# Gate and up products of three feed-forward blocks: one product of 512 columns for the upper weights, parts added outside PSUM

## The chip, the cores and the metric

One Trainium2 chip, one of its cores. The metric is the device time of one execution in microseconds, as the median of several executions. The whole program is one launch; all engines work on one example of 256 tokens.

## The reference, cut to what matters

Two blocks of two layers each run one after the other on `x` (256 tokens of width 1024). Three of the feed-forward parts in it are plain gated blocks, and these are the ones touched:

```python
def swiglu(xn, w_gu, w_down):                      # first block, layer 0
    g, u = jnp.split(xn @ w_gu, 2, axis=-1)        # hidden width 2816
    return (jax.nn.silu(g) * u) @ w_down

# second block, both layers, hidden width 2816
xn = _rms_norm(x, ffn_norm[l])
gate = _causal_dwconv(xn @ ffn_w_gate[l], ffn_conv_w[l], ffn_conv_b[l])
x = x + (jax.nn.silu(gate) * (xn @ ffn_w_up[l])) @ ffn_w_down[l]
```

The rest (mixers, attention, a mixture of eight experts) is not touched.

## The kernel before, in words

All data is float32. To use the fast reduced type of TensorE (float32r) without its loss of precision, each operand is split into an upper half (the value rounded to float32r) and a lower half (the rest), and a product is the sum of three: upper weights with upper input, upper weights with lower input, lower weights with upper input (`passes`). A weight block of 128x2048 arrives by DMA in one of four `raw` buffers; ScalarE copies it to its upper half `wH` (`act_blocks`, the copy is L229), then VectorE subtracts to get the lower half `wL` (`dve_blocks`, L200). There are three buffers of halves, so a block's halves can only be written when TensorE has finished the block three places back. Both functions work three blocks ahead of the tag they are called with.

A gated block is `pe_glu` on TensorE, `act_glu` on ScalarE and `dve_glu` on VectorE. It goes over the hidden width in 11 rounds of 256 channels. Round r on TensorE is: gate product (`pe_two`, L796), up product (`pe_two`), then the down product of round r-1 (L780; the last one is `pe_down_last`, L806). Weight blocks come in the same order: gate r, up r, down r-1. In `pe_two` the weights are stationary (128x128) and the input is moving (256 tokens): for each of 2 column halves j and 8 chunks c of the width there are three products of 256 columns, 48 in all. Gate or up of a round fill one PSUM bank of 512 columns, half j at columns 256j. The banks of these products are taken in turn from the four of the span (4, 8); banks 0 to 3 hold the sum of the down products. `bank` makes TensorE wait for the instruction that freed the bank last time: `dve_two`, which reads the bank, multiplies by the token scale `inv` and writes to SBUF.

VectorE's order in a round (`dve_glu`): weight halves that are due, gate scale (and in the second block three convolution taps, `dve_conv_gate`), up scale, product with the silu output, lower half of the hidden values (`hid_lo`), next weight halves. ScalarE's order (`act_glu`): `act_blocks` for the gate and up tags, `mid` (the silu), upper half of the hidden values (`hid_hi`), `act_blocks` for the down tag. In round 0 there is one more `act_blocks((*s, 1, 0))` ahead of `mid`: by it ScalarE prepares the block of the first down product, which takes the buffer that the up product of round 0 uses.

The first gated block is named `ffn1`, the two of the second block `("ffn2", 0)` and `("ffn2", 1)`. Other work is hooked onto rounds: in `ffn1` after round 4 the normalisation of the memory for the next layer (`pe_stat`, `dve_norm_memory_1`), after round 7 a small product (`pe_taps`); in `("ffn2", 0)` after round 5 another normalisation (`act_memory_in`, `dve_memory_in`).

The normalised input `X8` lies in one tensor `ra`: upper half of chunk c at column 256c, lower half 2560 columns further on.

Of the kernel before, what the change touches and what calls it, by code (L numbers as in the profile page):

```python
# [10 lines left out]
ALU = mybir.AluOpType  # L11
# [5 lines left out]
C = D // 128  # L17
# [234 lines left out]
def passes(wh, wl, xh, xl):  # L252
    return [(wh, xh), (wh, xl), (wl, xh)]


class Program:
# [497 lines left out]
    def pe_glu(self, p, s, n, x, x_ready, total, hooks={}):  # L754
        s = s if isinstance(s, tuple) else (s,)
        p.span = (4, 8)
        for r in range(n + 1):
            if r < n:
                for half in range(2):
                    out = self.bank(p, (*s, "gu"[half], r), self.dve, (*s, "scaled", "gu"[half], r))  # L760
                    self.pe_two(p, (*s, r, half), out, x, x_ready, (*s, "gu"[half], r), r == 0 and half == 0)
                    if r == 0 and half == 0:
                        p.span = (0, 4)
                        self.pe_total(p, total)
                        p.span = (4, 8)
            if r:
                q, tag = r - 1, (*s, r - 1, "down")
                wh, wl = self.pe_block(p, tag, 2)
                hv = self.hidden(s, q)
                p.wait_ge(*self.dve.of((*s, "hid_lo", q)))  # L770
                if q == n - 1:
                    self.pe_down_last(p, s, q, tag, wh, wl, hv)
                    continue
                for c in range(2):
                    for nb in range(8):
                        if q == 0 and c == 0 and nb % 2 == 0:
                            self.wait_bank(p, nb // 2, self.dve, (s[0] if len(s) == 1 else s, "res", nb + 1))
                        ns = slice(nb * 128, (nb + 1) * 128)
                        for i, (a, b) in enumerate(passes(wh[:, c, ns], wl[:, c, ns], hv[0][:, c, :], hv[1][:, c, :])):
                            m = p.op.matmul(self.banks[nb // 2][:, (nb % 2) * 256:(nb % 2) * 256 + 256], a, b,  # L780
                                            start=q == 0 and c == 0 and nb % 2 == 0 and i == 0,
                                            stop=False, skip_group_check=True)
                m.then_inc(*self.pe.up((*s, "down", q), ("block", self.index[tag])))
            if r in hooks:
                hooks[r](p)
        p.span = (0, 8)

    def pe_two(self, p, tag, out, x, x_ready, done, by_chunk):

        wh, wl = self.pe_block(p, tag, 8)  # L790
        order = [(j, c) for c in range(C) for j in range(2)] if by_chunk else [(j, c) for j in range(2) for c in range(C)]
        for j, c in order:
            js = slice(j * 128, (j + 1) * 128)
            p.wait_ge(*x_ready(c))
            for i, (a, b) in enumerate(passes(wh[:, c, js], wl[:, c, js], x[0][:, c, :], x[1][:, c, :])):
                m = p.op.matmul(out[:, j * 256:j * 256 + 256], a, b, start=c == 0 and i == 0 and not (j and by_chunk),  # L796
                                stop=c == C - 1 and i == 2, skip_group_check=by_chunk)
        m.then_inc(*self.pe.up(done, ("block", self.index[tag])))

    def pe_down_last(self, p, s, q, tag, wh, wl, hv):  # L800

        for nb in range(8):
            ns = slice(nb * 128, (nb + 1) * 128)
            for c in range(2):
                for i, (a, b) in enumerate(passes(wh[:, c, ns], wl[:, c, ns], hv[0][:, c, :], hv[1][:, c, :])):
                    m = p.op.matmul(self.banks[nb // 2][:, (nb % 2) * 256:(nb % 2) * 256 + 256], a, b, start=False,  # L806
                                    stop=c == 1 and i == 2, skip_group_check=True)
            if nb % 2:
                m.then_inc(*self.pe.up((*s, "out", nb // 2), *([(*s, "down", q), ("block", self.index[tag])] if nb == 7 else [])))
# [754 lines left out]
    def act_glu(self, a, s, n, mid, total, hooks={}):  # L1564
        for r in range(n + 1):
            if r < n:
                for half in range(2):
                    self.act_blocks(a, (*s, r, half))
                    if r == 0 and half == 0:
                        self.act_total(a, *total)  # L1570
                if r == 0:
                    self.act_blocks(a, (*s, 1, 0))
                mid(a, r)
                hv = self.hidden(s, r)
                if r > 1:
                    a.wait_ge(*self.pe.of((*s, "down", r - 2)))
                a.wait_ge(*self.dve.of((*s, "prod", r)))
                a.cp((*s, "hid_hi", r), hv[0], self.prod[:, r % 2, :].rearrange("p (c t) -> p c t", c=2))
            if r:
                self.act_blocks(a, (*s, r - 1, "down"))  # L1580
            if r in hooks:
                hooks[r](a)

    def act_gate(self, s):
        def mid(a, r):
            at = slice(2 * (r % 2), 2 * (r % 2) + 2)
            a.wait_ge(*self.dve.of((*s, "scaled", "g", r)))
            a.do((*s, "silu", r), self.sil[:, at, :], self.sil[:, at, :], ACT.Silu)
        return mid

    def act_conv_gate(self, s):
        def mid(a, r):
            at = slice(2 * (r % 2), 2 * (r % 2) + 2)
            a.wait_ge(*self.dve.of((*s, "conv", 2 * r + 1)))
            a.do((*s, "silu", r), self.sil[:, at, :], self.cvo[:, at, :], ACT.Silu)
        return mid
# [670 lines left out]

    def dve_two(self, v, s, which, r, dst):

        v.wait_ge(*self.pe.of((*s, which, r)))  # L2270
        v.tt((*s, "scaled", which, r), dst, self.ps((*s, which, r))[:, :].rearrange("p (j t) -> p j t", j=2),
             self.inv[:, :].unsqueeze(1).broadcast_to([128, 2, 256]), ALU.mult)

    def dve_conv_gate(self, s):
        l = s[1]
# [1128 lines left out]
```

## Time and profile before

| | us |
|---|---|
| median of 3 runs | 2411.12 (2410.07 to 2414.41) |
| profiled execution | 2420.16 |
| its span, first to last instruction | 2418.4 |
| TensorE busy | 2350.4 (97%) |
| VectorE busy | 1794.1 (74%) |
| ScalarE busy | 1368.9 (57%) |
| mean granted TensorE clock | 0.990 |

The profiled execution took 9.0 us more than the median; its span is what the views of the trace divide up. Times of day in the views count from the start of the span. "Busy" of TensorE's matmuls overlaps, as they are pipelined: what a product costs is the distance from start to start, read from a run of them in the chain of waits.

### The profile page before, as it was taken

The page shows a single profiled execution, that of the slowest core. Times are in us where ns is not written, and L with a number is a line of the kernel's source. Part 1 is how long each engine was busy: PE and PEld are TensorE (multiplying, and loading weights), DVE is VectorE, ACT ScalarE, POOL GpSimd, SP SyncE. Part 2 cuts the span into 40 slices and gives each one's busy share as a digit, 9 for nine tenths or more (in the row PEclk, how much of TensorE's full clock was granted, in tenths as well). Part 3 has the DMA queues.
Part 4 walks back from the last instruction along what each step waited for, and adds up shares of the span by engine and source line. Part 5 has one row for each costly group of instructions (what it writes and reads, how often), then busy time and mean ns, then how long its engine had stood idle before and what let it go on. Part 6 is the DMA issues. An engine that isn't in the chain of part 4 may idle for free.

```text
span 2418.4 us, 33634 instructions
## 1 busy us (share of the span) xinstructions
PE 2350.4 (97%) x14448; PEld 2095.7 (87%) x14448; DVE 1794.1 (74%) x1835; ACT 1368.9 (57%) x1348; POOL 117.5 (5%) x94
## 2 busy tenths in 40 slices
PE   6999999999999999999999999998999999999999
PEld 6999999788988888888888888887889999888999
DVE  4856566676788888888888888885767676766666
ACT  3535444464577776776767777775544444544433
POOL 3001000001100000000000000000210001301000
PEclk9999999999999999999999999999999999999999
DMA  7553546463499999999999999995333555433553
GB/s 228 175 192 124 182 162 207 138 200 122 153 360 349 361 339 346 348 348 343 350 343 349 350 348 368 332 366 193 114 112 116 192 192 173 122 108 102 192 175 105
DMA packets 309693, 566.91 MB, mean 234 GB/s; under 512 B 12387, under 2 KB 137602, under 8 KB 309409
## 3 DMA queue, kind: packets, MB, share of 16 engines
q1 hardware_dynamic: 304752, 559.34, 66.8%
q10 hardware_dynamic: 4784, 5.35, 0.7%
q8 instruction: 116, 1.90, 0.3%
q14 instruction: 41, 0.33, 0.0%
HBM read 563.60 MB, written 1.05 MB: 233 GB/s over the span
## 4 chain that ended last, share of the span: by engine, by line
PE 78%; DVE 9%; DMA 7%; ACT 4%; issue 1%; POOL 1%; ACTq 0%; DVEq 0%; POOLq 0%
PE bank L1005 18%; PE bank L796 15%; PE bank L1023 9%; PE bank L645 9%; PE bank L780 7%; PE bank L633 6%; DVE wL L200 5%; PE bank L248 5%; DMA raw<-in_od_moe_gu 5%; ACT wH L229 3%; PE bank L655 2%; PE bank L1293 2%; PE bank L1345 2%; PE bank L621 1%; DMA raw<-in_od_moe_down 1%; DVE arena L200 1%
## 5 line engine op out<-in xcount | busy, mean ns | idle before, releaser
L200 DVE TENSOR_TENSOR wL<-raw,wH 128x2048 fp32r<-128x2048 f32 (+2 forms) x544 | 1210.2, 2232 | 377.0 <-ACT wH L229 374.3
L229 ACT ACTIVATE wH<-raw 128x2048 fp32r<-128x2048 f32 (+2 forms) x544 | 1014.6, 1867 | 523.6 <-DMA raw<-in_od_moe_gu 113.8
L1005 PE MATMUL bank<-wH,ra 128*128 128x512 f32 x1792 | 579.1, 394 | 4.5 <-DVE wL L200 3.6
L1005 PEld LDWEIGHTS bank<-wH,ra 128*128 128x128 f32 x1792 | 336.5, 188 | 80.4 <-DVE wL L200 8.3
L796 PE MATMUL bank<-ra,wH 128*128 128x256 f32 x2112 | 383.7, 284 | 5.4 <-DVE ra L203 5.4
L1005 PE MATMUL bank<-wL,ra 128*128 128x512 f32 x896 | 349.0, 389 | 0.0
L796 PEld LDWEIGHTS bank<-ra,wH 128*128 128x128 f32 x2112 | 329.5, 192 | 8.1 <-DVE ra L203 6.9
L796 PE MATMUL bank<-ra,wL 128*128 128x256 f32 x1056 | 298.8, 283 | 0.0
L1023 PE MATMUL bank<-wH,ra 128*128 128x512 f32 x896 | 288.8, 393 | 4.1 <-DVE ra L200 3.2
L645 PE MATMUL bank<-wH,ra 128*128 128x512 f32 (+2 forms) x800 | 225.7, 364 | 4.9 <-DVE ra L203 4.9
L1023 PEld LDWEIGHTS bank<-wH,ra 128*128 128x128 f32 x896 | 168.8, 188 | 42.5 <-DVE wL L200 3.7
L796 PEld LDWEIGHTS bank<-ra,wL 128*128 128x128 f32 x1056 | 202.6, 192 | 0.0
L633 PE MATMUL bank<-ra,wH 128*128 128x256 f32 x1056 | 194.2, 286 | 7.7 <-DVE wL L200 4.0
L1005 PEld LDWEIGHTS bank<-wL,ra 128*128 128x128 f32 x896 | 168.5, 188 | 32.5
L633 PEld LDWEIGHTS bank<-ra,wH 128*128 128x128 f32 x1056 | 167.2, 195 | 9.1 <-DVE wL L200 4.6
L1023 PE MATMUL bank<-wL,ra 128*128 128x512 f32 x448 | 174.8, 390 | 0.0
L780 PE MATMUL bank<-ra,wH 128*128 128x256 f32 x960 | 174.2, 283 | 0.2 <-DVE wL L200 0.2
L645 PEld LDWEIGHTS bank<-wH,ra 128*128 128x128 f32 x800 | 149.7, 200 | 24.9 <-DVE ra L203 5.5
L633 PE MATMUL bank<-ra,wL 128*128 128x256 f32 x528 | 150.7, 286 | 0.0
L780 PEld LDWEIGHTS bank<-ra,wH 128*128 128x128 f32 x960 | 149.7, 192 | 0.4 <-DVE wL L200 0.4
L645 PE MATMUL bank<-wL,ra 128*128 128x512 f32 (+2 forms) x400 | 144.3, 361 | 0.0
L780 PE MATMUL bank<-ra,wL 128*128 128x256 f32 x480 | 135.8, 283 | 0.0
(212 smaller groups left out, 2561.8 us busy)
## 6 DMA issues: line engine op xcount, KB each, us to landing
raw<-in_od_moe_gu SPq DMA_DIRECT2D x224, 1024.0 KB, 6.8
raw<-in_od_moe_down SPq DMA_DIRECT2D x112, 1024.0 KB, 6.9
raw<-in_ev_ffn_gu SPq DMA_DIRECT2D x22, 1024.0 KB, 5.1
raw<-in_ffn_w_gate SPq DMA_DIRECT2D x22, 1024.0 KB, 5.6
raw<-in_ffn_w_up SPq DMA_DIRECT2D x22, 1024.0 KB, 5.3
raw<-in_ffn_w_down SPq DMA_DIRECT2D x22, 1024.0 KB, 5.0
raw<-in_xa_wkv SPq DMA_DIRECT2D x16, 1024.0 KB, 5.2
raw<-in_od_pw_w SPq DMA_DIRECT2D x12, 1024.0 KB, 5.1
```

What stands on the lines that cost most here:

```text
L200: self.op.tensor_tensor(out, a, b, op).then_inc(*self.sig.up(name))
L229: self.op.activation(out, a, ACT.Copy, **kw).then_inc(*self.sig.up(name))
L248: m = self.op.matmul(out, a, b, start=i == 0, stop=i == len(pairs) - 1)
L633: m = p.op.matmul(out, a, b, start=c == 0 and i == 0, stop=c == k - 1 and i == 2)
L645: m = p.op.matmul(outs[t][:, 0:wd], a, b, start=half == 0 and c == 0 and i == 0, stop=half == 1 and c == 3 and i == 2)
L655: m = p.op.transpose(out[place], part, self.ident[0:count, 0:count])
L780: m = p.op.matmul(self.banks[nb // 2][:, (nb % 2) * 256:(nb % 2) * 256 + 256], a, b, start=q == 0 and c == 0 and nb % 2 == 0 and i == 0, s ...
L796: m = p.op.matmul(out[:, j * 256:j * 256 + 256], a, b, start=c == 0 and i == 0 and not (j and by_chunk), stop=c == C - 1 and i == 2, skip_ ...
L1005: m = p.op.matmul(out[:, :], a, b, start=half == 0 and c == 0 and i == 0, stop=half == 1 and c == 3 and i == 2)
L1023: m = p.op.matmul(self.banks[n][:, :], a, b, start=f == 0 and half == 0 and c == 0 and i == 0, stop=f == NRD - 1 and half == 1 and c == 1 ...
L1293: i = p.op.matmul(out[:, m, :], one, other, start=first, stop=False, skip_group_check=True)
L1345: m = p.op.matmul(self.banks[nb // 2][:, (nb % 2) * 256:(nb % 2) * 256 + 256], one, other, start=first and c == 0 and nb % 2 == 0 and i == ...
```

## The change

In `pe_two` the two products that share the upper weights become one of 512 columns: its moving operand is a view of `ra` with two pieces of 256 columns, 2560 apart (`both`). It writes a whole bank, so each of the two column halves j has a bank of its own: columns 0 to 255 hold upper-by-upper, and the product with the lower weights is added there; columns 256 to 511 hold upper-by-lower. ScalarE copies columns 256 to 511 of each bank to the destination in SBUF (`act_parts`), VectorE adds columns 0 to 255 to it, and then multiplies by the token scale in SBUF. The core of the diff:

```diff
@@ pe_glu
-                    out = self.bank(p, (*s, "gu"[half], r), self.dve, (*s, "scaled", "gu"[half], r))
-                    self.pe_two(p, (*s, r, half), out, x, x_ready, (*s, "gu"[half], r), r == 0 and half == 0)
+                    outs = [self.bank(p, (*s, "gu"[half], r, j), self.dve, (*s, "sum", "gu"[half], r, j)) for j in range(2)]
+                    self.pe_two(p, (*s, r, half), outs, x, x_ready, (*s, "gu"[half], r), r == 0 and half == 0)
@@ pe_two
-            for i, (a, b) in enumerate(passes(wh[:, c, js], wl[:, c, js], x[0][:, c, :], x[1][:, c, :])):
-                m = p.op.matmul(out[:, j * 256:j * 256 + 256], a, b, start=c == 0 and i == 0 and not (j and by_chunk),
-                                stop=c == C - 1 and i == 2, skip_group_check=by_chunk)
+            p.op.matmul(outs[j][:, :].rearrange("p (h t) -> p h t", h=2), wh[:, c, js], self.both(c), start=c == 0, stop=False,
+                        skip_group_check=True)
+            m = p.op.matmul(outs[j][:, 0:256], wl[:, c, js], x[0][:, c, :], start=False, stop=c == C - 1, skip_group_check=True)
+    def both(self, c):
+        return self.ra[:, 256 * c:256 * c + 5120].rearrange("p (h t) -> p h t", h=2)[:, :, 0:256]
@@ act_glu, after mid(a, r)
+                if r > 1:
+                    a.wait_ge(*self.dve.of((*s, "hid_lo", r - 2)))
+                self.act_parts(a, s, "u", r, self.prod[:, r % 2, :].rearrange("p (j t) -> p j t", j=2))
+    def act_parts(self, a, s, which, r, dst):
+        a.wait_ge(*self.pe.of((*s, which, r)))
+        for j in range(2):
+            a.cp((*s, "part", which, r, j), dst[:, j, :], self.ps((*s, which, r, j))[:, 256:512])
@@ act_gate, act_conv_gate: first statement of mid, ahead of the silu
+            self.act_parts(a, s, "g", r, self.sil[:, at, :])          # act_gate
+            self.act_parts(a, s, "g", r, self.gpad[:, at, 2:258])     # act_conv_gate
@@ dve_two
-        v.wait_ge(*self.pe.of((*s, which, r)))
-        v.tt((*s, "scaled", which, r), dst, self.ps((*s, which, r))[:, :].rearrange("p (j t) -> p j t", j=2),
-             self.inv[:, :].unsqueeze(1).broadcast_to([128, 2, 256]), ALU.mult)
+        for j in range(2):
+            v.wait_ge(*self.act.of((*s, "part", which, r, j)))
+            v.tt((*s, "sum", which, r, j), dst[:, j, :], dst[:, j, :], self.ps((*s, which, r, j))[:, 0:256], ALU.add)
+        v.own()
+        v.tt((*s, "scaled", which, r), dst, dst, self.inv[:, :].unsqueeze(1).broadcast_to([128, 2, 256]), ALU.mult)
```

## Rows read from the trace of the kernel before

**Rows 1.** The page: busy time by engine; the chain that ended last, by engine.
```profile
PE 2350.4 (97%) x14448; PEld 2095.7 (87%) x14448; DVE 1794.1 (74%) x1835; ACT 1368.9 (57%) x1348; POOL 117.5 (5%) x94
PE 78%; DVE 9%; DMA 7%; ACT 4%; issue 1%; POOL 1%; ACTq 0%; DVEq 0%; POOLq 0%
```

**Rows 2.** Busy time in the three stages: PE, PEld, DVE, ACT, POOL, PEclk, DMA.
```profile
217.30:410.00 192.70, 192.49 (x1567) 189.17 (x1566) 117.10 (x110) 86.80 (x75) 2.04 (x2) 1.00 0.55 184
1857.00:2041.40 184.40, 184.40 (x1539) 184.36 (x1537) 134.24 (x157) 78.75 (x64) 0.00 (x0) 1.00 0.57 184
2230.60:2416.00 185.40, 184.39 (x1537) 184.19 (x1535) 128.18 (x150) 71.94 (x54) 0.00 (x0) 1.00 0.48 158
```

**Rows 3.** Chain of waits in order of time: start us, us, what.
```profile
711.96 5.46 PE bank L1005 x24
...
1943.41 5.76 PE bank L780 x48
1949.17 11.52 PE bank L796 x96
```

**Rows 4.** Timeline of VectorE, one round of ("ffn2", 0): start us, us, instruction.
```profile
1939.69 2.29 DVE L200 TENSOR_TENSOR wL<-raw,wH 128x2048 fp32r<-128x2048 f32 x1 [3.46 <-ACT wH L229]
1941.90 0.68 DVE L200 TENSOR_TENSOR arena<-bank,rs 128x512 f32<-128x512 f32 x1
1942.62 0.74 DVE L209 TENSOR_SCALAR arena<-arena,cols 128x256 f32<-128x256 f32 x2
...
1944.86 0.69 DVE L200 TENSOR_TENSOR arena<-bank,rs 128x512 f32<-128x512 f32 x1
1945.65 0.69 DVE L200 TENSOR_TENSOR arena<-arena 128x512 f32<-128x512 f32 x1
1947.04 0.69 DVE L200 TENSOR_TENSOR ra<-arena,ra 128x512 fp32r<-128x512 f32 x1 [0.70 <-ACT ra L229]
1948.84 2.29 DVE L200 TENSOR_TENSOR wL<-raw,wH 128x2048 fp32r<-128x2048 f32 x1 [1.11 <-ACT wH L229]
```

**Rows 5.** Timeline of ScalarE, the same round.
```profile
1937.74 1.92 ACT L229 ACTIVATE wH<-raw 128x2048 fp32r<-128x2048 f32 x1 [3.84 <-PE bank L796]
1944.97 0.63 ACT L226 ACTIVATE arena<-arena 128x512 f32<-128x512 f32 x1 [5.31 <-DVE arena L203]
1946.91 1.90 ACT L229 ACTIVATE wH<-raw 128x2048 fp32r<-128x2048 f32 x1
```

**Rows 6.** Groups by line and form: ScalarE in 183:195, VectorE in 2410:2419.
```profile
L229 ACT ACTIVATE sq<-bank 128x256 f32<-128x256 f32 x3 | 1.2, 384 | 1.7 <-PE bank L655 1.7
...
L200 DVE TENSOR_TENSOR hT<-hT,bank 128x256 f32<-128x256 f32 x8 | 3.0, 418 | 5.0 <-PE bank L806 5.0
```

**Rows 7.** Timeline of VectorE, after the end of ("ffn2", 0).
```profile
2039.83 2.73 DVE L200 TENSOR_TENSOR hT<-hT,bank 128x256 f32<-128x256 f32 x8
```

**Rows 8.** Chain of waits, first rounds of ("ffn2", 0).
```profile
1857.02 17.27 PE bank L796 x144
```

**Rows 9.** Timeline of ScalarE, round 0 of ("ffn2", 0).
```profile
1862.87 1.92 ACT L229 ACTIVATE wH<-raw 128x2048 fp32r<-128x2048 f32 x1 [3.53 <-PE bank L796]
```

**Rows 10.** Timeline of VectorE: hooked work in ("ffn2", 0); last hid_lo of ("ffn2", 1).
```profile
1951.05 3.25 DVE L203 SCALAR_TENSOR_TENSOR ra<-arena,cols,ra 128x256 fp32r<-128x256 f32 x8
...
2407.11 0.69 DVE L200 TENSOR_TENSOR ra<-arena,ra 128x512 fp32r<-128x512 f32 x1 [0.70 <-ACT ra L229]
```

**Rows 11.** Chain of waits: hooked work in ffn1; last down product.
```profile
298.54 3.47 PE bank L581 x16
...
311.37 2.30 DVE wL L200
...
2409.23 5.77 PE bank L806 x48
```

**Rows 12.** Timeline of ScalarE, round 4 of ffn1: upper half of a weight block, squares of the hook.
```profile
294.87 1.90 ACT L229 ACTIVATE wH<-raw 128x2048 fp32r<-128x2048 f32 x1
296.68 2.18 ACT L226 ACTIVATE sq<-arena 128x512 f32<-128x512 f32 x4
```

More of the change, by code:

```diff
@@ L786, in pe_glu, with pe_two @@
         p.span = (0, 8)
-    def pe_two(self, p, tag, out, x, x_ready, done, by_chunk):
+    def pe_two(self, p, tag, outs, x, x_ready, done, by_chunk):
         wh, wl = self.pe_block(p, tag, 8)
```

## The prediction, made before the changed kernel was run

> **What bounds the kernel now.** I read the page first: TensorE is busy 97% of the span and holds 78% of the chain that ended last [rows 1]. Then the busy times of the three stretches that the change touches: TensorE has no gap in them, at full granted clock, while VectorE is busy 61 to 73% and ScalarE 39 to 45% [rows 2]. So here TensorE's own stream sets the end; the chain shows it as runs of L796 and L780 that follow each other without a piece of another engine between them [rows 3]. The reader should see that neither transfers (share 0.48 to 0.57) nor the other engines are late, but by how much they are not late is in no such view. That I read from the timelines of VectorE and ScalarE in one round [rows 4, 5].
>
> **Gain on TensorE.** 48 products of 256 columns take 5.76 us, 120 ns each; 24 of 512 columns, in the expert stage, take 5.46 us, 227.5 ns each [rows 3]. A pair (j, c) cost 3 x 120 = 360 ns and will cost 227.5 + 120 = 347.5: 12.5 ns less. That is 16 x 12.5 = 0.20 us for a gate or up product (5.56 for 5.76), and a round becomes 5.56 + 5.56 + 5.76 = 16.88 us for 17.28. There are 66 such products; the first gate product of each ffn2 stage follows VectorE chunk by chunk and gains nothing. 64 x 0.20 = **12.8 us**.
>
> No row has a moving operand in two pieces, nor 512 and 256 columns in alternation. Bounds: the 512 costs as two of 256 (pair 360, gain 0); or all beyond the columns themselves vanishes for the 256 (107 ns at 2.4 GHz, pair 334, gain 27). I take 347.5, as both lengths show the same surplus of 13 to 14 ns over their columns.
>
> The Trainium skill, "TensorE: Matmul & The Clock Gate", section "Back-to-back issue gap", gives an isolated gap of N/2.4 + 2.5 ns. By it the merger would save 2.5 ns a pair, an estimate of 2.6 us in all instead of 12.8; the rows show a surplus five times as large, and the sum goes by them.
>
> **Added work.** Per gate or up: two copies on ScalarE of 128x256 out of PSUM, 0.38 us each [rows 6], and two additions on VectorE, 0.42 each, but 0.33 from start to start, since eight in a row take 2.73 [rows 7]. ScalarE instructions also overlap by some 0.1 us, so a second copy ends 0.28 after the first. The scale, now SBUF to SBUF, stays at 0.69, as the arena<-arena row has it [rows 4]. Busy time: VectorE +1.6 us a round on some 12, ScalarE +1.5 on 7, under a round of 16.88. What matters is latency.
>
> *The chain of a steady round in ffn2.* Count from the end of a gate product (1937.65, the L780 start at 1943.41 less one up product [rows 3]). Before: wH copy to +2.0, wL from +2.04, scale +4.25, taps +4.97, silu +7.32, up scale +7.21, product +8.0, wH of the next up block +9.26, its wL ends at 1951.13 = +13.48 [rows 4, 5]. TensorE wants that block at 1949.17 + 5.76 = 1954.93, +17.28: 3.8 us to spare. With the change:
> - Gate: sums at +4.25 and +4.58, done +4.99, scale +5.04, taps +5.76: 0.8 later. The copies (+1.9 to +2.6) are hidden.
> - Up: the copies stand behind the silu on ScalarE, which waits for the taps: silu +8.11, copies done +9.02 and +9.32, sums +9.06 and +9.39, scale +9.85, product +10.64 for +8.0.
> - So everything behind it is 2.64 later: wL of the up block ends at +16.12 and is wanted at +16.88. **0.75 us to spare**: no stall in a steady round, but the cover is nearly gone. In ffn1 (no taps) the wH copy stood at +7.84 (294.87, the gate ending 11.52 before L581 starts at 298.54 [rows 11, 12]) and the cover was 5.2. There the sums wait for the up product's end and the copies behind it: copies +6.3 to +7.0, sums to +7.45, wH copy at +9.53, and 3.1 remain.
>
> **Where the cover is missing.** Here the new waits reach TensorE.
>
> (a) *Round 0 of all three stages.* The four banks of the span now hold one gate and one up product instead of four. The gate product of round 1 therefore needs the banks of gate 0, freed by its sums; these wait for the ScalarE copies; and the copies are in `mid`, behind `act_blocks((*s, 1, 0))`, whose wH copy waits until the up product of round 0 ends (idle 3.53 for L796 [rows 9]). Behind up 0's end: wH copy 0.09 to 2.01, parts to 2.57, sums to 3.06, TensorE goes on at 3.12. Before, it needed no wait (144 products in 17.27 us [rows 8]). 3 x 3.1 = **9.3 us**.
>
> (b) *Rounds 1 and 2 of ffn2.* Same origin: scale at 3.10, taps to 6.15, wL of the first down block to 8.35, sums of up 0 to 9.00; up 1 wanted the banks at 8.68 and gets them at 9.06: 0.4. The wH copy of gate 2 starts only at 11.09, after hid_hi 0, wL at 13.02, and 14.08 later (16.12 less 2.04) the wL of up 2 is done: 27.10; TensorE wants it at 9.06 + 16.88 = 25.94: 1.2. By round 3 the 0.75 is back. 2 x 1.6 = **3.2 us**. In ffn1 the chain is shorter by the taps and nothing follows.
>
> (c) *The last down product of ffn2.* It has no products of a next round before it. hid_lo ended at 2407.80, TensorE began L806 at 2409.23 [rows 10, 11], 1.4 to spare. Now hid_lo is 2.64 later and TensorE 0.2 earlier behind the gate's end: 1.45 late with the hand-over. 2 x 1.45 = **2.9 us**. In ffn1 hid_lo has room.
>
> (d) *Hooked work.* ("ffn2", 0): 3.2 us of VectorE behind the wL of the up block [rows 10] now push the next chain by 2.5, less 0.75: 1.8. ffn1, round 4: squares start 1.69 later than 296.68 [rows 12], so L581, which ran 3.47 from the down product's end, ends 0.5 later; the 11.65 from its end (302.01) to the end of wL (311.37 + 2.30) [rows 11] are followed by TensorE now 0.4 earlier, and one round later the up block is 0.35 late: 1.2. Sum **3.0 us**.
>
> Sum: -12.8 + 9.3 + 3.2 + 2.9 + 3.0 = **+5.6 us**: the profiled execution, 2420.16 with its span of 2418.4, would be 2425.8. It lies 9.0 above the median of the runs, which goes from 2411.1 to **2416.7**.
>
> The Trainium skill, "Perfetto Trace Analysis", section "Matmuls", says that independent groups should go round through different PSUM banks, so that one's evacuation lies beside the next one's products, and also that larger matmuls are more efficient. The change takes the second at the cost of the first, and no wait for a bank is in the rows before; (a) is where I expect one.
>
> **The rivals.**
>
> *Faster: the pair is cheaper than the sum of its rows.* Place: the weight load of the 256-column product, which would go wholly under the 512 columns before it. At 334 ns a pair the gain is 0.42 us a product, 27; the steady cover sinks to 0.3, and (b) to (d) grow by some 1.5: 27 - 20 = 7 us faster, 2404. It decides from a pair of 342 ns (even) and 337 (0.2% faster). For it: loads are listed beside products throughout. Against: 512-column products, whose loads had the most room, still cost 14 ns over their columns.
>
> *Slower: the chain of ffn2 outgrows its round.* If copies, sums and their waits take 1.5 us more than I count, 0.75 is added in each of 8 rounds of both stages (12) and 1.5 at each of five places in (b) to (d) (7.5): 2436. Against it: all terms but the hand-overs between engines (0.03 to 0.1 in the rows) are measured durations.
>
> *No gain: 512 in two pieces costs as two products.* Pair 360, gain 0; with rounds of 17.28 the terms (b) to (d) fall to some 7, (a) stays at 9: 2427. This is also about what the page's gap above would give.
>
> *Round 0 does not stall*, because the order of ScalarE is not as I read it: (a) and (b) drop, 12.5 us: 2404.
>
> **How the numbers follow.** Forecast as worked out, 0.65; cheaper pair 0.08; no stall in round 0 0.04; outgrown chain 0.11; no gain 0.07; else 0.05. The latencies in (b) to (d) rest on one chain, and 0.3 us in it moves the sum by about 2; with the spread of the runs my own range for the forecast is 2411 to 2422. What a measurement can tell from no change is about 0.2%, 4.8 us: 2406.3 to 2415.9. The forecast lies just beyond it, so of its 0.65 I give 0.33 to slower and 0.32 to same. With the rivals: slower 0.52, same 0.35, faster 0.13. The range, 2407 to 2427, leaves out the faster cases and the outgrown chain.
>
> **What would show it.** Per stage, a gap of some 3 us on TensorE ahead of the second gate product, released by a VectorE sum, with ScalarE's wH copy and two part copies before that; 24-odd pairs at 347 to 348 ns in between; runs of 32 products for L796 in 5.56 us; in ffn2 short waits for wL in round 2 and for hid_lo ahead of the last L806, but none in rounds 4 and 6 to 10. A wait for wL in every round would show the outgrown chain; no gap in round 0 would refute (a), the largest loss, and pairs under 342 ns the gain.

## The result, and the profile after

| | before | after |
|---|---|---|
| median, alternated on one chip (7 runs each) | 2413.31 us (2407.61 to 2418.68) | 2423.79 us (2419.96 to 2431.04) |
| ratio, 95% interval | | 1.0057 (1.0044 to 1.0070) |
| profiled execution, its span | 2420.16, 2418.4 | 2423.79, 2422.0 |

The change makes the kernel slower by 10.6 to 16.9 us: the medians are 10.5 apart, and the ratio puts the change at 13.8. The forecast had 5.6: the sign was right and the main gaps lie where it put them, but the size is off by more than a factor of two.

The page after: busy time by engine, and the two groups into which L796 has split.

```profile
PE 2343.7 (97%) x13392; PEld 2042.0 (84%) x13392; DVE 1843.9 (76%) x1967; ACT 1403.7 (58%) x1480; POOL 116.7 (5%) x94
...
L796 PE MATMUL bank<-ra,wH 128*128 128x512 f32 x1056 | 382.7, 405 | 16.5 <-DVE arena L200 9.6
...
L798 PE MATMUL bank<-ra,wL 128*128 128x256 f32 x1056 | 299.4, 283 | 0.0
```

Against [rows 1], TensorE has 1056 products fewer and is even busy 6.7 us less, in a kernel that takes longer. What counts is on the right: its idle time ahead of L796 has a new releaser, the VectorE sums, with 9.6 us.

The two executions can't be compared by their spans. They differ by 3.6 us, but from the last down product of `ffn1` to the first product of `("ffn2", 0)`, in code that the change doesn't touch, the one of after happened to be 9.3 us shorter. So I measured each stage in each kernel: from the first product for the token scale (L589) to the start of the last down product, both read from the timeline of TensorE. (A piece in the chain of waits begins where the one before it ends, and products overlap: the chain has the last down product of `("ffn2", 1)` of before at 2409.23 [rows 11], the timeline its first product at 2409.07. The table goes by the timeline throughout.)

| us | ffn1 | ffn2, 0 | ffn2, 1 | sum | against before |
|---|---|---|---|---|---|
| before | 186.67 | 178.98 | 178.98 | 544.63 | |
| after | 191.19 | 185.44 | 183.16 | 559.79 | +15.2 |

15.2 agrees with the interval of the ratio, and this table is the measure for all that follows.

The waits of TensorE in `("ffn2", 0)`: who waited for whom, us in total, times, the longest.

```profile
PE bank L796 <- DVE arena L200: 3.2, 1, 3.2
PE bank L811 <- DVE ra L200: 1.4, 1, 1.4
PE bank L796 <- DVE wL L200: 1.4, 1, 1.4
```

Three waits, and no more: (a) once, (c) once, and the hooked work once. `("ffn2", 1)` has the first two, with the same figures; `ffn1` has the 3.2, 0.6 for the squares of the hook and 0.4 for one wL. (These waits are counted from the end of the last product. From start to start each costs up to 0.15 more, as the next product would have begun before that end.) Here is the gap of `ffn1` in the chain of waits: start, us, what.

```profile
226.79 0.13 PE bank L798
227.01 1.91 ACT wH L229
228.92 0.28 ACT arena L229
229.22 0.76 DVE arena L200 x2
229.99 0.14 issue
230.12 0.77 PE bank L796
230.89 0.21 PE bank L798
231.10 0.43 PE bank L796
231.53 0.21 PE bank L798
...
236.61 0.23 PE bank L796
236.84 0.12 PE bank L798
```

The first five lines are term (a) as it was foretold: the up product ends, ScalarE first makes the upper half of a weight block, only then the part copies, then come the sums, and TensorE goes on after 3.2 us. The lines behind them the forecast did not have: a product of 512 columns at 0.43 us and one of 256 at 0.21, for 0.23 and 0.12 from 236.61 on. The granted clock of these stretches (start:end, length, busy times of PE, PEld, DVE, ACT, POOL, then the clock, DMA share and GB/s), first behind the gap and then further on, for the three stages in turn:

```profile
230.10:236.20 6.10, 6.08 (x19) 5.23 (x20) 5.33 (x7) 2.47 (x5) 0.00 (x0) 0.50 0.38 123
236.60:240.00 3.40, 3.40 (x22) 2.99 (x21) 0.00 (x0) 1.22 (x1) 0.00 (x0) 1.00 0.23 76
1858.66:1864.30 5.64, 5.64 (x17) 4.83 (x18) 5.60 (x10) 1.82 (x4) 0.00 (x0) 0.50 0.05 20
1864.50:1869.00 4.50, 4.50 (x28) 3.89 (x27) 2.07 (x3) 2.43 (x2) 0.00 (x0) 1.00 0.75 235
2239.70:2243.50 3.80, 3.80 (x15) 3.20 (x13) 3.80 (x7) 1.18 (x3) 0.00 (x0) 0.55 0.02 4
2243.70:2249.00 5.30, 5.30 (x32) 4.60 (x31) 3.42 (x7) 2.89 (x4) 0.00 (x0) 1.00 0.64 198
```

The clock stands at 0.50 (1.2 GHz) behind each of the three gaps and then returns to 1.00 (2.4 GHz). A pair takes 0.64 us there for 0.35. By the timeline it is, from the first product behind the gap to the first of the down product, 13.95, 13.93 and 12.92 us, for 11.31 in a steady round. So the slow clock costs 2.6, 2.6 and 1.6 us: 6.9 in all, over two thirds of what the gaps themselves cost. In the same places of before the clock is 1.00 and 144 products take 17.27 us [rows 8].

The rounds that follow. Starts of the down products of four neighbouring rounds in the chain of waits of `("ffn2", 0)`:

```profile
1872.75 5.76 PE bank L780 x48
...
1889.62 5.75 PE bank L780 x48
...
1906.68 5.75 PE bank L780 x48
...
1923.75 5.75 PE bank L780 x48
```

From start to start: 16.87, 17.06 and 17.07. Less 5.76, gate and up take 11.11 us in the first and 11.31 in the others, that is 347 and 353.4 ns for each of their 32 pairs. The first is the forecast's figure, and only three whole rounds of the kernel have it.

The timeline of VectorE in one round, to be laid beside [rows 4], and under it that of ScalarE, beside [rows 5]:

```profile
1937.20 2.29 DVE L200 TENSOR_TENSOR wL<-raw,wH 128x2048 fp32r<-128x2048 f32 x1 [0.86 <-ACT wH L229]
1939.41 0.75 DVE L200 TENSOR_TENSOR arena<-arena,bank 128x256 f32<-128x256 f32 x2
1940.19 0.69 DVE L200 TENSOR_TENSOR arena<-arena,rs 128x512 f32<-128x512 f32 x1
...
1944.20 0.75 DVE L200 TENSOR_TENSOR arena<-arena,bank 128x256 f32<-128x256 f32 x2 [0.97 <-ACT arena L229]
...
1948.91 2.29 DVE L200 TENSOR_TENSOR wL<-raw,wH 128x2048 fp32r<-128x2048 f32 x1 [1.11 <-ACT wH L229]
```
```profile
1943.27 0.63 ACT L226 ACTIVATE arena<-arena 128x512 f32<-128x512 f32 x1 [5.56 <-DVE arena L203]
1943.80 0.64 ACT L229 ACTIVATE arena<-bank 128x256 f32<-128x256 f32 x2
```

From one wL to the next it is 11.71 us, 14.00 to its end; the forecast's chain had 14.08. The idle 0.97 is VectorE waiting for the part copies of up, which stand behind the silu. And in the steady rounds nobody on TensorE waits, as forecast: cover was left, and a little more than planned for, since the round lasts 17.06 and not 16.88.

### The profile page after: what moved, and what is told of

Its sections match the earlier page's. It is cut to its first block, busy times and chain, and to the rows that moved or that the text cites. A ratio compares the mean times of both kernels' runs of the same rounds, so it can differ in the third digit from the quotient of the medians.

```text
span 2422.0 us, 31781 instructions
## 1 busy us (share of the span) xinstructions
PE 2343.7 (97%) x13392; PEld 2042.0 (84%) x13392; DVE 1843.9 (76%) x1967; ACT 1403.7 (58%) x1480; POOL 116.7 (5%) x94
## 3 DMA queue, kind: packets, MB, share of 16 engines
q8 instruction: 106, 1.74, 0.3%
HBM read 563.60 MB, written 1.05 MB: 233 GB/s over the span
## 4 chain that ended last, share of the span: by engine, by line
PE 79%; DVE 10%; DMA 5%; ACT 5%; issue 1%; POOL 1%; ACTq 0%; DVEq 0%; POOLq 0%
PE bank L1010 20%; PE bank L1028 10%; PE bank L796 9%; PE bank L645 9%; PE bank L633 7%; PE bank L780 6%; PE bank L248 5%; DVE wL L200 5%; PE bank L798 4%; ACT wH L229 3%; DMA raw<-in_od_moe_gu 3%; PE bank L655 2%; DVE arena L200 2%; PE bank L1298 2%; PE bank L1350 2%; PE bank L621 1%
## 5 line engine op out<-in xcount | busy, mean ns | idle before, releaser
L796 PE MATMUL bank<-ra,wH 128*128 128x512 f32 x1056 | 382.7, 405 | 16.5 <-DVE arena L200 9.6
L796 PEld LDWEIGHTS bank<-ra,wH 128*128 128x128 f32 x1056 | 201.8, 191 | 69.1 <-DVE arena L200 10.5
L633 PE MATMUL bank<-ra,wH 128*128 128x256 f32 x1056 | 193.6, 286 | 10.2 <-DVE wL L200 6.4
L633 PEld LDWEIGHTS bank<-ra,wH 128*128 128x128 f32 x1056 | 166.8, 194 | 11.6 <-DVE wL L200 7.0
L780 PE MATMUL bank<-ra,wH 128*128 128x256 f32 x960 | 174.0, 283 | 0.4 <-DVE wL L200 0.4
L780 PEld LDWEIGHTS bank<-ra,wH 128*128 128x128 f32 x960 | 149.3, 191 | 2.2 <-DVE wL L200 0.7
L780 PE MATMUL bank<-ra,wL 128*128 128x256 f32 x480 | 135.8, 283 | 0.0
```

The lines of the kernel that those rows point to most:

```text
L633: m = p.op.matmul(out, a, b, start=c == 0 and i == 0, stop=c == k - 1 and i == 2)
L796: p.op.matmul(outs[j][:, :].rearrange("p (h t) -> p h t", h=2), wh[:, c, js], self.both(c), start=c == 0, stop=False, skip_group_check=True)
```

## The experiments

The questions were: what does the gap of round 0 cost with all that hangs on it; is the slow clock an effect of the gap or of the new products; why does a pair take 353 ns; and what does the merger bring by itself. Each kernel ran beside the kernel before on the same chip.

### Part copies of round 0 ahead of the weight block

```diff
@@ act_glu, r == 0
                 if r == 0:
+                    parts(a, 0)                       # act_parts(a, s, "g", 0, ...)
                     self.act_blocks(a, (*s, 1, 0))
@@ mid of act_gate and act_conv_gate
-            self.act_parts(a, s, "g", r, ...)
+            if r:
+                parts(a, r)
```

> The changed kernel with one move: in round 0 ScalarE makes the two part copies of the gate product ahead of the upper half of the first down block. Theory (the gap ahead of the second gate product comes from ScalarE's order, and the half clock behind it comes from the gap): no wait of TensorE for a VectorE sum in round 0, granted clock 1.0 in the whole of rounds 0 to 2 of all three stages, and about 15 us less than the changed kernel: 0 to 3 us below the kernel before (ratio 0.999 to 1.000). Rival 1 (two groups of two banks are too few whatever the order): a gap of over 1 us stays there. Rival 2 (the slow pairs of round 1 come from the products themselves): the gap goes, but pairs of 0.64 us stay, ratio about 1.003.

2411.62 us (12 runs) against 2410.06 (17), ratio 1.0005 (0.9993 to 1.0017): with two copies moved in one order the kernel can't be told from the one before. The stages are 187.11, 180.97 and 179.50, in sum +2.9 over before and 12.2 below after. The 15 us that were expected back did not come in full. The gaps are gone, and so is the slow clock; the stretches are the first 22 to 24 us of each stage:

```profile
223.00:245.00 22.00, 22.00 (x142) 19.84 (x141) 15.97 (x20) 11.97 (x17) 0.00 (x0) 1.00 0.59 191
1845.00:1868.00 23.00, 22.95 (x145) 20.33 (x144) 19.91 (x31) 9.94 (x15) 0.00 (x0) 1.00 0.59 183
2218.00:2242.00 24.00, 23.94 (x150) 21.17 (x149) 20.21 (x32) 10.84 (x17) 0.00 (x0) 1.00 0.54 175
```

Of the 16.7 us of gaps and slow clock 12.2 come back. Of the rest, 1.5 is the wait for wL in round 2 of both ffn2 stages, 0.8 and 0.7, which appears now that TensorE arrives in time. It stands where term (b) put its larger part; in the changed kernel TensorE is late there itself. Another part, 1.5, is a lowered clock late in `ffn1` (0.88 to 0.93 in the 18 us around L827), which neither before nor after has. The last down products still wait 1.4 each, and rounds still take 17.06.

### A gap alone, without any merger

Two kernels keep the products of before, with 256 columns, and only make TensorE wait ahead of the second gate product: for the upper half of the first down block, or for the scaled up product, which comes later.

```diff
@@ pe_glu, kernel before
                 for half in range(2):
+                    if r == 1 and half == 0:
+                        p.wait_ge(*self.act.of(("w_hi", self.index[(*s, 0, "down")])))    # short
+                        p.wait_ge(*self.dve.of((*s, "scaled", "u", 0)))                   # long, in its place
```

> The kernel before with one wait added: in round 1 of each stage TensorE waits, ahead of the gate product, for the upper half of the first down block on ScalarE, a gap of about 2.0 us behind the up product of round 0. No other change, products of 256 columns. If the half clock behind the gap needs a gap like the 3.2 us of the changed kernel, no product runs slow here and the three stages take 6 us more in all; if any idle of a few us brings it, the products behind the gap take 0.24 us for some us and the stages take 12 us or so more. If slow products belong to the changed kernel's products alone, none here.

> The kernel before with one wait added: in round 1 TensorE waits, ahead of the gate product, for the scaled up product of round 0 on VectorE, a gap of about 5 us. Theory (idle time brings the half clock): products of 256 columns go at about 0.21 to 0.24 us instead of 0.12 for 3 to 7 us behind the gap in at least two of three stages, stages 15 us more by the gaps and 5 to 9 by the clock. Rival (the slow pairs come from the products of 512 columns): products at 0.12 throughout, 15 us more.

One run each, 2421.75 and 2432.73 us, for 2410.06. The waits measure 2.1 and 5.0 us in every stage. What tells is the run of 96 products right behind them in the chain of waits, which takes 11.52 at full clock [rows 3]; first the short gap, then the long one, in the order of the stages:

```profile
229.86 13.27 PE bank L798 x96
...
1858.68 11.78 PE bank L798 x96
...
2236.28 13.26 PE bank L798 x96
```
```profile
234.45 13.41 PE bank L798 x96
...
1867.43 14.30 PE bank L798 x96
...
2245.86 14.48 PE bank L798 x96
```

So products of 256 columns fall to the low clock just as well. Behind the short gap the second stage kept the full clock, and its run takes 0.3 more than 11.52 all the same. Against this 11.78, the low clock costs 1.5 us in each of the other two, and behind the long gap 1.6, 2.5 and 2.7. The slow clock belongs to the gap, not to the merged product. The sums of the stages agree: +11.4 for 6.2 us of short gaps, +24.0 for 15.0 of long ones, with 1.5 in each for a lowered clock late in `ffn1`.

The Trainium skill, "Perfetto Trace Analysis", section "Matmul Optimizations", has the rule for it: the engine scales its power with its utilisation, so matmuls should be issued back to back, in batches. The traces agree, down to a pause of 2.1 us between stretches of which each is busy at 2.4 GHz. I had not weighed it in the prediction.

### Why 353 ns a pair and not 347

Two causes were possible: the moving operand in two pieces, or the alternation of two lengths. The first kernel takes one contiguous piece of 512 columns, the upper halves of two neighbouring chunks, so what is summed up is another number than in the reference; only the times count here. The second keeps the two pieces but issues eight products of 512 and then eight of 256, for each half j.

```diff
@@ both: one piece
-        return self.ra[:, 256 * c:256 * c + 5120].rearrange("p (h t) -> p h t", h=2)[:, :, 0:256]
+        return self.ra[:, 256 * max(c - 1, 0):256 * max(c - 1, 0) + 512].rearrange("p (h t) -> p h t", h=2)
@@ pe_two: grouped
-            m = p.op.matmul(outs[j][:, 0:256], wl[:, c, js], x[0][:, c, :], ...)
+            if c == C - 1:
+                for k in range(C):
+                    m = p.op.matmul(outs[j][:, 0:256], wl[:, k, js], x[0][:, k, :], ...)
```

> The changed kernel, but the moving operand of the 512-column product is one piece of 512 neighbouring columns (upper halves of two neighbouring chunks: other numbers, same sizes). Theory A (the two-piece view costs the 6 ns by which a pair is dearer than its rows): a pair takes 347.5 ns, a gate or up product 5.56 us. Theory B (the change of length from 512 to 256 and back costs it): a pair stays at 353 ns, 5.655 us a product. The gap and half clock of round 0 stay in both.

> The changed kernel, with the order of the products in a column half j changed: first the eight of 512 columns, then the eight of 256 (in the first gate product too, where half j follows chunk by chunk). Theory A (the two-piece view is what costs): 8 products of 512 take 8 x 233 ns, and 8 of 256 take 8 x 120, a gate or up product still 5.65 us. Theory B (the change of length costs): 8 x 227.5 and 8 x 120, 5.56 us a product. The waits of round 0 stay.

One run each, 2429.36 and 2420.88. With one piece the down products start as far apart as before the edit, 17.06:

```profile
1893.82 5.75 PE bank L780 x48
...
1910.88 5.75 PE bank L780 x48
...
1927.94 5.75 PE bank L780 x48
```

The view in two pieces costs nothing. Grouped, the chain of waits shows the two lengths apart:

```profile
1888.30 5.76 PE bank L780 x48
1894.06 1.84 PE bank L796 x8
1895.89 0.95 PE bank L800 x8
...
1905.23 5.76 PE bank L780 x48
```

A round is 16.93, gate and up 11.17, or 349 ns a pair. Two thirds of the excess over 347 go with fewer changes of length. Neither expectation had this value between 347.5 and 353. Why some products of the changed kernel take 347 all the same remains open. Its timeline shows where they are: 11 of the 66 run at 347 in all but their first pairs, none of them more than four gate or up products behind a wait, a stretch of low clock or products of another kind. Further away it was 353.4 throughout.

### The merged product taken apart again

```diff
@@ pe_two
-            p.op.matmul(outs[j][:, :].rearrange("p (h t) -> p h t", h=2), wh[:, c, js], self.both(c), ...)
+            for h in range(2):
+                p.op.matmul(outs[j][:, 256 * h:256 * h + 256], wh[:, c, js], x[h][:, c, :], ...)
```

> The changed kernel with the banks, the part copies and the sums as they are, but the merged product taken apart again into two of 256 columns (columns 0 to 255 and 256 to 511 of the same bank): the extra work without the gain. If a pair's saving is what the merger brings, three products take 360 ns again, a gate or up product 5.76 us, the steady round 17.28 us, and the three stages are 6 to 7 us longer than in the changed kernel; gap and half clock of round 0 stay. If the saving came from the banks, the round stays at 17.06.

2429.58 us in one run, for 2410.3 before. All that the change adds is there (gaps of 3.2, the copies, the sums), without its gain. Gate and up are back at 11.52. The stages sum to 565.09: +20.5 over before, +5.3 over after. So the added work costs about 20 us. The 5.3 is the merger's gain with two accidents of the clock in it: here the gap of `("ffn2", 0)` was followed by full clock, which spared the 2.6 us that the changed kernel lost there, and in `ffn1` the clock was 0.83 from 358 to 368, which cost some 1.5. Set against each other they bring it to about 6.4, and `("ffn2", 1)`, which has neither, differs by 2.2, or 6.5 for three stages: near the 6.7 that 353.4 ns a pair give for the 63 products between the marks. The stage with full clock behind the gap has one thing more: a wait of 0.4 for wL at the up product of round 2, where the forecast had (b).

### Both orders mended

On top of the first experiment the part copies of up stand ahead of the silu as well, which had kept them and the sums behind it waiting for the convolution.

```diff
@@ act_glu, after mid(a, r)
-                if r > 1:
-                    a.wait_ge(*self.dve.of((*s, "hid_lo", r - 2)))
-                self.act_parts(a, s, "u", r, ...)
@@ mid of act_gate and act_conv_gate, ahead of the wait for the silu's input
+            self.act_up(a, s, r)                      # the three lines above
```

> The changed kernel with two moves on ScalarE: in round 0 the gate's part copies ahead of the upper half of the first down block, and in every round the up product's part copies ahead of the silu. Theory: no gap in round 0, and the chain from gate to the next up weights is 1.1 us shorter in the second block, so the waits for the weights behind the hooked work and for the last hidden values shrink from 1.4 us to about 0.3 each; gain of 6.8 us on TensorE less some 2 us of waits: 4 to 6 us below the kernel before, ratio 0.998. Rival (the late chain is set by VectorE alone, the silu's place does not matter): as with the first move alone, ratio 0.9995 to 1.000.

2403.74 us (12 runs) against 2409.35 (17), ratio 0.9972 (0.9959 to 0.9986): faster than before. Stages 188.21, 177.61, 177.60, in sum 1.2 below before, though in this execution a lowered clock late in `ffn1` cost about 3. TensorE's waits in `("ffn2", 0)`:

```profile
PE bank L811 <- DVE ra L200: 0.4, 1, 0.4
PE bank L796 <- DVE arena L200: 0.2, 1, 0.2
```

The 1.4 ahead of the last down product is down to 0.4, and both waits for wL, (b)'s and the hook's, have gone; in `ffn1` one of 0.6 ahead of L780 remains. So the up chain's wait for the silu was behind (b), (c) and the larger part of (d).

### All products of 512 columns first

On top of that, both halves j of upper weights come first, sixteen products, then the sixteen with the lower weights, and TensorE waits for wL only ahead of these.

```diff
@@ pe_two, not by_chunk
+            p.wait_ge(*self.act.of(("w_hi", self.index[tag])))
+            for j in range(2):
+                for c in range(C):
+                    ...
+                    p.op.matmul(outs[j][:, :].rearrange("p (h t) -> p h t", h=2), wh[:, c, j * 128:(j + 1) * 128], self.both(c), ...)
+            p.wait_ge(*self.dve.of(("w_lo", self.index[tag])))
+            for j in range(2):
+                for c in range(C):
+                    m = p.op.matmul(outs[j][:, 0:256], wl[:, c, j * 128:(j + 1) * 128], x[0][:, c, :], ...)
```

> The kernel with both moves on ScalarE (part copies ahead of the first down block and of the silu), and on TensorE, but for the first gate product, all sixteen products of 512 columns of a block first, then the sixteen of 256, with the wait for the lower weights only ahead of these. Theory (a change of length costs some 5 to 6 ns a pair; the lower weights are then wanted 3.7 us later): a gate or up product takes 5.57 us, no wait for wL is left in the three stages, only some 0.5 us for the last hidden values in the second block; gain 12 us less 2: 9 to 11 us below the kernel before, ratio 0.995 to 0.997. Rival (the grouping brings nothing, as the wait for hidden values takes it): ratio as with the two moves alone, 0.997 to 0.998, and a steady round over 17.0 us.

2398.41 us (6 runs, 2392.91 to 2400.93) against 2410.30 (11), ratio 0.9950 (0.9932 to 0.9967): faster than both kernels, 12 us below before. One product and the next in the chain of waits:

```profile
1884.00 3.65 PE bank L797 x16
1887.66 1.91 PE bank L802 x16
1889.57 3.65 PE bank L797 x16
1893.22 1.91 PE bank L802 x16
1895.14 5.76 PE bank L780 x48
```

228 and 119 ns, so 347 a pair, now in every round: the very sum of [rows 3] that the forecast had used. The stages sum to 535.80, 8.8 less than before. One wait for wL is left, 0.6 in `ffn1` ahead of a down product; the expectation had none.

## Why the prediction was right in kind and wrong in size

Term by term, over the three stages:

| us | forecast | measured |
|---|---|---|
| gain of 64 products | -12.8 | -7.3 |
| (a) gaps of round 0 | +9.3 | +9.8 |
| clock behind these gaps | none | +6.9 |
| (b) rounds 1 and 2 | +3.2 | 0 |
| (c) last down product | +2.9 | +3.1 |
| (d) hooked work | +3.0 | +2.7 |
| sum | +5.6 | +15.2 |

All is measured from start to start. The gain is 63 x 16 x (360 - 353.4) ns = 6.7, as the first gate product of `ffn1` lies ahead of the marks, and 0.2 for each of the three cheap rounds. (a) is 3.26 a stage and (c) 1.53. In (d), 1.5 is in ffn2, where the round with the hook takes 18.55 for 17.07, and 1.05 and 0.2 are in two neighbouring rounds of ffn1.

**Mis-sized: the gain.** The step that failed is the one that took 347.5 ns for a pair, "as both lengths show the same surplus". Each length had been measured in a run of its own kind, and nothing had shown them in alternation, as the text said itself. The bounds were 334 and 360, and the value lay near the middle of them. It costs 5.5 us of the 9.6 by which the sum is off. The experiments put it down to the order: 353 alternating one by one, 349 by eights, 347 by sixteens, and the same 353 with a contiguous operand. The rule of the Trainium skill that the prediction quotes ("TensorE: Matmul & The Clock Gate", section "Back-to-back issue gap") would have given an estimated gain of 2.6 us; the runs lie between it and the forecast.

**Missing: the clock.** The sum treated a gap on TensorE as its own length. Behind the three gaps the granted clock was 0.50 for some microseconds, which cost 6.9 us in all. That two kernels with the old products lose 1.5 to 2.7 us to the clock in five of six such gaps shows that this term comes with (a) and not with the merger. A term of the right name and size would have been 3.2 + 2.3 a stage.

**Right: (a).** Place, releaser and length (3.12 forecast, 3.2 measured) are as worked out from ScalarE's order, and the first experiment shows the cause: two copies moved, and it is gone.

**Hidden: (b).** The step assumed TensorE in time after the gap. In the two ffn2 stages it was 2.6 and 1.6 us late through the clock, and the wL of round 2 was ready. The kernel taken apart has one such stage with the gap and without the slow clock, and there the wait appears: 0.4, where the step's own working gives 0.8 for its rounds of 17.28 (27.10 less 9.06 + 17.28). With the gap taken away it is 0.7 and 0.8. The 0.4 a stage at up 1 shows in no list of waits. Two wrong steps offset each other by 3 us, which made the total look closer than the reasoning was.

**Right: (c), (d) and the steady rounds.** 1.53 a stage for 1.45; 1.5 and 1.25 for 1.8 and 1.2; a chain of 14.00 for 14.08, and no waits in the steady rounds. (The step for (c) took TensorE's start from the chain, 2409.23; with the timeline's 2409.07 it would have had 1.6.) Since the cover counted on was 0.75 with a round of 16.88, the slower pair gave back 0.18 of cover in each round, which is part of why (d) came out smaller in ffn2.

**The rivals.** The cheaper pair, the outgrown chain and "round 0 does not stall" are refuted by the rows. "No gain" priced the total best (2427, for a ratio that makes 2424.9 of 2411.12), but for the wrong reason: half of the gain was there, and the clock took it.

What stays open: what gives some products 347 ns in the changed kernel; why the clock falls behind one gap of 2.1 or 3.2 us and not behind another; and what costs 1.5 us in the last kernel. There 63 x 0.195 = 12.3 us of gain and 2.0 of waits for wL and hidden values (0.6, 0.5 and 0.5, with 0.15 each from start to start) would give 10.3, and the stages give 8.8. Of the 1.5, 1.3 lies ahead of the first down products: they start 17.30, 17.72 and 17.69 us behind the mark, where the steady pace would give 17.13.

## What to carry to other kernels

Where a change makes accumulators last longer or gives each product more banks, walk through the first round, not the steady one: what frees the banks there, and what stands ahead of it in the order of the engine that empties them. A gap on an otherwise busy TensorE has a price of its own length and, for the gaps of 2.1 to 5.0 us here, mostly another 1.5 to 2.7 us for the clock. And when two products of different length replace three of one, issue them in groups by length and put the copies that free banks ahead of everything that waits for a longer chain: here these two orders turned a loss of 14 us into a gain of 12.

## What the runs showed of the hardware

- The clock fell to 0.50 behind gaps of 2.1 us in 2 of 3 cases, behind 3.2 in 11 of 12 (the changed kernel, the one with a contiguous operand, the grouped one, and all but one stage of the one taken apart), behind 5.0 in 3 of 3. In these stages no gap of 0.9 to 1.6 lowered it; behind the 1.4 ahead of a last down product, in the changed kernel, it stands so:

```profile
2034.75:2040.70 5.95, 5.95 (x49) 5.95 (x50) 4.98 (x4) 2.74 (x2) 0.00 (x0) 1.00 0.24 62
```

- At the low clock a pair takes 640 ns, exactly its 768 columns at 1.2 GHz; at the full clock 347 to 353 for 320. The surplus of [rows 3] exists only there.
- 2.1 us is no lower bound. In code that the change doesn't touch, the kernel before has a wait of 1.74 us at 2097.8; TensorE was busy all of the 7.8 us ahead of it at 1.00, and from 2100.1 to 2103.5 the clock was 0.50.
- It can fall without a wait. In the kernel with both orders mended it was 0.81 from 350 to 368 us, around the eight small products of L827, which took 4.45 us for 3.58, and no wait of TensorE is listed near. Before, after, the one with a contiguous operand and the last kernel had 1.00 there, the other six traces a lowered clock that set in at or right behind these eight products. I did not pursue it.
